# Reordering the first step of a gated conv-FFN, and one weight rounding of every step

## The reference

```python
def _conv_ffn(h, w_up, conv_w, conv_b, w_down):
    z = h @ w_up
    u, v = z[..., :D_FF], z[..., D_FF:]          # D_FF = 3072
    u = _dwconv(u, conv_w, conv_b, (1, 1))       # width 3, per channel, over tokens
    return (gelu(u) * v) @ w_down
```

## Time and profile before

| | |
|---|---|
| median of 3 runs | 2213.75 us (2208.13 to 2214.6) |
| profiled execution | 2208.13 us, span 2205.9 us |
| PE busy | 2067.2 us, 94% of the span |
| DVE busy | 1515.3 us, 69% |
| POOL busy | 1277.6 us, 58% |
| ACT busy | 804.9 us, 36% |
| mean granted clock of PE | 0.962 |

### The profile page before, as it was taken

One profiled execution on the slowest core, in us unless ns is written; L12 is line 12 of the kernel. 1 busy time (PEld: TensorE's weight loads), 2 busy tenths in 40 slices (PEclk: granted clock), 3 DMA queues, 4 the chain that ended last, 5 costly groups with the idle time before them and its releaser, 6 DMA issues.

```text
span 2205.9 us, 26602 instructions
## 1 busy us (share of the span) xinstructions
PE 2067.2 (94%) x9064; PEld 1678.1 (76%) x9064; DVE 1515.3 (69%) x1521; ACT 804.9 (36%) x1062; POOL 1277.6 (58%) x818
## 2 busy tenths in 40 slices
PE   7899998878899999999999969799999999999996
PEld 7577775666688888888888758677888888888885
DVE  6688887248877777777777784784666555665557
ACT  3475666226223232222323345453222322223322
POOL 1433233255777877778777543457667666667653
PEclk9999998988999999999999979799999999999998
DMA  6132321231122222222222320201111111111114
GB/s 277 67 114 76 119 71 63 105 123 49 67 91 90 76 85 86 86 87 75 86 95 86 124 77 20 86 29 48 57 57 48 48 48 57 57 50 45 49 46 152
DMA packets 52121, 174.94 MB, mean 79 GB/s; under 512 B 4816, under 2 KB 5104, under 8 KB 50928
## 3 DMA queue, kind: packets, MB, share of 16 engines
q1 hardware_dynamic: 52080, 174.41, 22.6%
HBM read 161.80 MB, written 12.58 MB: 79 GB/s over the span
## 4 chain that ended last, share of the span: by engine, by line
PE 79%; DVE 8%; ACT 7%; issue 3%; POOL 2%; DMA 0%; ACTq 0%; POOLq 0%; SPq 0%; DVEq 0%
PE ps L729 38%; PE ps L476 32%; PE ps L608 3%; PE ps L843 1%; PE ps L515 1%; DVE V L1495 1%; ACT TH L1006 1%; PE ps L551 1%; PE ps L810 1%; DVE Y L1582 1%; DVE Y L1595 1%; PE ps L831 1%; DVE T_lo L1885 1%; PE ps L573 1%; ACT RA L1012 1%
## 5 line engine op out<-in xcount | busy, mean ns | idle before, releaser
L1802 DVE TENSOR_TENSOR Y<-Y,ps 128x1024 f32<-128x1024 f32 x336 | 409.9, 1221 | 54.5 <-PE ps L476 14.3
L1403 POOL TENSOR_TENSOR F_lo<-S,F_hi 128x1024 fp32r<-128x1024 f32 x44 | 107.4, 2440 | 375.4 <-ACT F_hi L1111 375.4
L476 PE MATMUL ps<-F_hi,WC_hi 128*128 128x512 f32 x736 | 231.2, 392 | 6.7 <-DVE Y L1802 4.0
L476 PE MATMUL ps<-F_hi,WC_lo 128*128 128x512 f32 x736 | 229.7, 390 | 0.0
L1082 ACT ACTIVATE S<-S 128x1024 f32<-128x1024 f32 x48 | 50.9, 1060 | 484.7 <-DVE S L1897 484.7
L904 ACT ACTIVATE So_hi<-So_raw 128x512 fp32r<-128x512 f32 x132 | 82.6, 627 | 383.2 <-POOL So_raw L1293 383.2
L476 PE MATMUL ps<-F_lo,WC_hi 128*128 128x512 f32 x704 | 217.4, 390 | 0.0
L1377 POOL TENSOR_TENSOR So_lo<-So_raw,So_hi 128x512 fp32r<-128x512 f32 x132 | 188.7, 1458 | 1.5 <-ACT So_hi L904 1.5
L476 PEld LDWEIGHTS ps<-F_hi,WC_hi 128*128 128x128 f32 x736 | 138.3, 189 | 37.3 <-DVE Y L1802 4.5
L476 PEld LDWEIGHTS ps<-F_hi,WC_lo 128*128 128x128 f32 x736 | 138.4, 188 | 29.1
L476 PEld LDWEIGHTS ps<-F_lo,WC_hi 128*128 128x128 f32 x704 | 132.5, 188 | 28.0
(11 more groups left out here) (275 smaller groups left out, 5332.4 us busy)
## 6 DMA issues: line engine op xcount, KB each, us to landing
rawA<-wA SPq DMA_DIRECT2D x60, 512.0 KB, 3.3
rawB<-wB SPq DMA_DIRECT2D x60, 512.0 KB, 3.3
E<-ada SPq DMA_DIRECT2D x47, 512.0 KB, 3.3
rawC<-wC SPq DMA_DIRECT2D x46, 512.0 KB, 4.1
quad<-ada SPq DMA_DIRECT2D x8, 2048.0 KB, 9.7
ada_first<-ada SPq DMA_DIRECT2D x4, 2048.0 KB, 16.2
outT<-X SPq DMA_DIRECT2D x16, 512.0 KB, 2.8
X<-outT SPq DMA_DIRECT2D x16, 512.0 KB, 7.1
```

Of the source, the lines that this page charges most:

```text
L476: mm = pe.matmul(out, w[:, w_cols:w_cols + P], (hi, lo)[part], start=first and w is W_hi[s] and part == 0, stop=last and w is W_lo[s])
L1403: TT(dst[:], S[1][:], F_hi[:].bitcast(F32), ALU.subtract).then_inc(f_ready, 1)
L1802: TT(Y[:, m], Y[:, m], flat(ps[:, b:b + 2, :]), ALU.add).then_inc(d_added, 1)
```

## The change

It moves instructions within the streams of ACT, POOL and DVE; none is added or removed, and PE's and SP's streams stay as they are.

- ACT, first step: the rounding of the second W_B right behind `copy_u(0)`; `round_t(2)` ahead of the first gelu; `round_t(1)` ahead of `round_f(0)`.
- ACT, every step but a layer's last: the rounding of "22" for the next unit behind `gelu(j)` instead of ahead of it.
- POOL, first step: the remainder of the second W_B ahead of the ada product (layer 0) or of W_C's remainder (layer 1), and of F_lo.
- DVE, first step: all four of `T_raw[2]` ahead of the taps; the first gate product behind `T_raw[1]` instead of ahead of it; `right_lo(0)` and `ada_sum(1, 0)` ahead of `add_down(L, 0)`, where both stood behind it.

```diff
--- before.py
+++ after.py
@@ -1114,14 +1114,14 @@
 
                 round_second("A", L)
                 copy_u(L, 0, AB01)
+                round_second("B", L)
                 if L:
                     round_down(L, 0)
                 round_t(L, 0)
+                round_t(L, 2)
                 gelu(L, 0)
-                round_t(L, 2)
+                round_t(L, 1)
                 round_f(L, 0)
-                round_second("B", L)
-                round_t(L, 1)
                 copy_u(L, 1, AB23)
                 for name in ("S4", "S1", "11", "12", "S2"):
                     round_op(name, L, 2)
@@ -1154,9 +1154,9 @@
                     round_op("S2", L, j + 1)
                     round_op("S4", L, j + 1)
                     round_op("S3", L, j + 1)
-                    round_op("22", L, j + 1)
                 gelu(L, j)
                 if not last:
+                    round_op("22", L, j + 1)
                     return
                 act.preload_act_table(ACT.Sqrt)
                 act.wait_ge(op_done, done_at("22", t))
@@ -1379,12 +1379,12 @@
             def ffn_first(L):
 
                 lo_of_unit("A", N_STD + 2 * L + 1)
+                lo_of_unit("B", N_STD + 2 * L + 1)
                 if L:
                     lo_of_unit("C", DN * L)
                 else:
                     ada_product(2)
                 f_remainder(L, 0)
-                lo_of_unit("B", N_STD + 2 * L + 1)
                 for name in MADE_ORDER:
                     combine(name, L, 2)
                 for name in READY_FIRST[:5]:
@@ -1854,14 +1854,12 @@
                     minus(T_raw[0][k], Y[:, k, hs(1)], Y[:, k, hs(0)]).then_inc(t_raw, 1)
                 dve.wait_ge(x_saved[1], 64 * (L + 1))
                 for k in range(half):
-                    if k == 2:
-                        taps(L, 0)
                     if k % 2:
                         minus(T_raw[2][k], Y[:, k + half, hs(1)], Y[:, k, hs(1)]).then_inc(t_raw, 1)
                     else:
                         STT(T_raw[2][k], Y[:, k + half, hs(1)], dM[:, k:k + 1], Y[:, k, hs(1)],
                             ALU.add, ALU.subtract).then_inc(t_raw, 1)
-                gated(L, 0)
+                taps(L, 0)
                 dve.wait_ge(x_saved[0], 64 * (L + 1))
                 for k in range(half):
                     dve.wait_ge(t_raw, 16 * L + half + k + 1)
@@ -1870,6 +1868,7 @@
                     else:
                         STT(T_raw[1][k], Y[:, k, hs(0)], M[:, a + k:a + k + 1], T_raw[2][k],
                             ALU.add, ALU.add).then_inc(t_raw, 1)
+                gated(L, 0)
                 for k in range(half):
                     dve.wait_ge(t_raw, 16 * L + 2 * half + k + 1)
                     if k % 2:
@@ -1922,11 +1921,11 @@
                     dve.wait_ge(ada_out, NH + 2)
                     dve.reciprocal(cc[:, 1], ps[:, 0, 8:8 + 4 * KT]).then_inc(cols_step, 1)
                     add_ada_bias(ps[:, 0, 0:2], 48, 2, NH + 2)
-                add_down(L, 0)
+                right_lo(L, 0)
                 if L == 0:
                     ada_sum(1, 0)
+                add_down(L, 0)
                 taps(L, 1)
-                right_lo(L, 0)
                 right_lo(L, 1)
                 right_lo(L, 2)
```

## The result

The change makes the kernel slower: median 2306.0 us (2298.99 to 2309.41, 4 runs) against 2212.92 (2208.13 to 2214.6, 4 runs), a ratio of 1.042 with a 95% interval of 1.0391 to 1.045. By the medians that is 93.1 us. I had said 2275, from 2238 to 2303: the direction was right, the size 31 us short, and the time lies just outside the range.

What follows compares the result with a forecast made beforehand. TensorE was taken to bound the kernel, so edits cost only where they make PE stand. Rounding 54 us plus first-step reordering 12.5 made 66.5, added to the profiled 2208.13: 2275, range 2238 to 2303.

Steps and rivals of the forecast that it cites:

- layer 2's loop: Late "22" rounding in layer 2's feed-forward steps, which load no E: taken as 0, with 0 to 6 us.
- clock falls in most steps: Rival: layer 1's loop stalls also bring slow restarts, 1.7 us per step, 34 in all; 2292 to 2310, chance 0.12.
- part 2: Reordered first step, both layers: later first down product, partly regained in step 2; 9.8 − 2.2 + 8.5 − 3.6 = 12.5 us.
- The rounding in layer 1's loop: Layer 1, steps 3 to 22: late rounding delays rawB, E and the first add; 2.7 us per step, 54 us.
- The gains: Step 2 of both layers: shorter by 2.2 us in layer 1 and 3.6 us in layer 2.
- E in time: Rival: layer 1's loads come faster, hiding the rounding: 2221, half hidden 2247; chance 0.17 wholly or half.
- The other side, faster: Rival: first-step copies not delayed, layer 1's 7.33 us stall and 1.9 go, loads hidden: −9.2 us, 2199; chance 0.04.
- no effect: Rival: first-step gains balance losses and the loop's rounding is hidden: 2208 ± 6 us; chance 0.05.
- The figure of the Trainium skill: Layer 1's loop: about 358 GB/s from HBM, giving a 1.45 us stall per step and 29 us instead of 54.

Runs made afterwards that it cites:

- Run 1: The kernel before with only the "22" rounding moved behind the gelu in every step: 2302.38 us, 1.0406 of before.
- run 3: The changed kernel with SP's wait for "22" and rawB's load moved behind W_C's load and the first E load: 2211.64 us, 0.9991 of before.
- Run 9: The changed kernel with only W_C's load ahead of rawB, E's first load staying behind it: 2219.75 us, 1.0039 of before.
- run 2: The changed kernel with the "22" rounding back ahead of the gelu, leaving only the reordered first step: 2215.17 us, 1.0008 of before.
- run 4: The kernel before with SP issuing W_C's load and the first E load ahead of rawB: 2207.31 us, 0.9972 of before.
- run 8: The kernel of run 4 with DVE's four T_lo[2] remainders moved behind the second gate product: 2198.47 us, 0.9935 of before.
- run 10: The kernel of run 8 with T_lo[1] also behind the second gate product and T_lo[2] behind the first sum of u: 2203.18 us, 0.9957 of before.

## Why the prediction was right in direction and short in size

The measured 2306 lies 3 us above the range, and one term put it there: without the 21.3 that layer 2's loop cost and that I had taken as 0, it would be about 2285. It falls where I had put "clock falls in most steps" (2292 to 2310, 0.12), but only 5 of layer 1's 20 steps had one, so that is no success of that rival. One error ran the other way and hid some of the miss: part 2 came out 5.7 cheaper than I had it.

**The rounding in layer 1's loop: right, link by link.** In 15 of the 20 steps the granted clock over the step is 1.00; these average 33.64, against 33.6 on record. E's product starts at P + 12.2 to P + 13.7, on average P + 13.05. Runs 1 and 3 show that the rounding is the cause and SP's order the path.

**The clock: a rival that came true in part.** Five of the 20 steps (34.88 to 35.21) have a clock of 0.95 and average 35.04, 1.40 more each: 7.0 in all. With 20 × 2.71 this makes the 61.2. The two rows at the top show the pattern: 35.21 at 0.95 with 1.80 and 0.27 of stall, 34.13 at 1.00 with 1.83 and 0.82. Run 1 has six such steps of 34.8 to 35.3. I had priced all of them at 0, with 34 as the other bound.

**Layer 2's loop: the term that failed.** "I take 0, with 0 to 6 us for the layer" measured 21.3. The path was the one named, every size on it was small. POOL's remainder takes 2.02 in all 20 steps, so rawB goes out at P + 6.35, not 5.6: I had named the gate product's turn, up to 0.9, and left it out of the sum. rawC goes out 0.88 behind rawB, and W_C's rounding starts 3.9 to 5.0 behind that; the one instance that I used had 0.67 and 3.90. On average W_C's rounding starts at P + 11.75, where I had P + 10.17. Of these 1.58, 0.75 is the gate product's turn and the rest the two loads. About 0.8 of the 1.58 had been free; what is left, and a little slower restart, is 1.06 per step. A step's length follows the landing alone: W_C rounded at P + 11.09 gives 30.90, at P + 12.06 31.88, at P + 12.19 32.02. Run 9 takes W_C out of the queue behind the remainder and the 21.3 are gone. Twenty steps multiply a miss of 1 us by 20: the slack of 0.8 should have been set against the spread of the landing, not against one value.

The trace of the kernel before already held better values. In all 20 steps of its layer 1 rawC goes out 0.9 behind rawB, as it does here, and lands 4.4 to 4.9 behind its own issue, about 5.5 behind rawB's, where I used 4.57 up to the rounding. SP's queue at the start of step 3, and rawC's landing there (DMA issues, 615 to 625):

```profile
615.19 0.33 SPq L415 DMA_DIRECT2D rawB<-wB  x1
616.10 0.33 SPq L420 DMA_DIRECT2D rawC<-wC  x1
...
rawC<-wC SPq DMA_DIRECT2D x1, 512.0 KB, 4.6
```

**Part 2: the balance was right, its size was not.** I had 12.5; in the kernel after the first steps and steps 2 of both layers sum to 6.8, and run 2 gives 2.1 by the medians, within what can't be told from no change. In layer 1 the fourth tile starts 5.2 late (562.35 against 557.2), not 8.4: the T_lo took 7.32, not 5.4, but T_raw[3] was done at 551.5, not 556.6, so the copies start at 561.09. Two of V's subtractions had taken 2.91 and 2.87 beside POOL; now all took 0.69 to 0.75, and F_lo, which came later, took 3.56 instead of 3.00. In layer 2 the stall sits at F_lo (5.75) and the copies are covered by it (0.44), where I had put 7.0 on the copies. The gains were off too: step 2 gained 4.6 in layer 1, not 2.2, and 0.9 in layer 2, not 3.6; that step hangs on the same W_C load as the loop.

**What I did not see.** Layer 1's last step: E is late there too, and its last down product waits 3.50 for its left side where it waited 1.74 before. With the slower stretch behind it (granted clock at half from 1324.8 to 1328.2) the stage is 3.2 longer. The 2.3 between the layers stays open: it arises in layer 2's token mixer, which the change does not touch, and the kernel before was profiled in its fastest execution, 4.8 under its median.

**The rivals.** "E in time" is refuted by POOL's wait of 2.80 for E. "The other side, faster" and "no effect" both needed a hidden rounding, and the faster one T_lo that fit ahead of the copies; neither holds. The figure of the Trainium skill ("DMA: Bandwidth & Descriptors", section "Specifications"), by which E would land an estimated 6.4 behind rawB's issue, stood in the prediction with a time of 2250. In the trace E's product starts 6.6 to 8.0 behind rawB's issue, on average 7.4 (13.05 less 5.63), so the row was the better guide. The 2 us of fixed cost in the 6.4 stand in that page's section on loads issued by GpSimd ("Anatomy of one DMA — SWDGE (gpsimd) path"), and these loads are issued by SP; no run here splits a landing into its parts.

## What to carry to other kernels

A queue that issues in one written order and waits in it passes a wait on to all that stands behind it: before an operation is moved, look up which load waits for its result, and what is issued after that load. If the step of a loop has under 1 us of slack on such a path, take the latest landing that the trace shows and not the one that is at hand, and multiply the delay by the number of steps. Where an engine has more to do than its stage has room for, reordering moves the stall; the gain came from putting the load order right first (run 4), and then moving only the work that stood ahead of the operation PE waits for (run 8).

## What the runs showed of the hardware that I had not expected

- Equal stalls do not bring equal clocks. Four steps of the kernel after whose one stall was 1.60 to 1.82 took 32.86 to 33.29 at a granted clock of 1.00; three with one of 1.79 to 1.86 at the same place took 34.88 to 35.05 at 0.95, with part of the step at 1.2 GHz instead of 2.4. In the step from 617.74 PE restarted at 644.38 after a stall of 1.80, and the granted clock was at half from 645.5 to 648.9. What decides between the steps no row showed.
- A load's landing depends on its neighbours. In layer 2 of the kernel after rawC, second in the row, was rounded 3.9 to 5.0 behind its issue from step to step, with nothing else changed, and 4.4 to 5.9 in layer 1, where E follows it; E, third, was taken up 5.1 to 6.5 behind its issue, where it had landed in 3.3 when alone.
- DVE and POOL alternate over long stretches. T_lo took 0.63 each where POOL left room (three in 1.89, run 10); four took 7.32 beside F_lo and three combinations, and the combinations took 1.61 to 1.74 instead of 1.29: both engines pay.
